# Seven waits in a two-layer decoder kernel: three asked for later or by bank, two pieces of work moved ahead, the first loads and the last stores cut anew

## The reference, cut to what matters

```python
mem_n = rmsnorm(mem, mem_norm)
for layer in range(2):
    g = norms[layer]
    h = rmsnorm(x, g[0])
    mix = even_mixer(h, ...) if layer % 2 == 0 else odd_mixer(h, ...)
    x = x + rmsnorm(mix, g[1])
    h = rmsnorm(x, g[2])
    x = x + rmsnorm(memory_cross_attention(h, mem_n, ...), g[3])
    h = rmsnorm(x, g[4])
    x = x + rmsnorm(swiglu(h, ...), g[5])
```

## Time and profile before

| | us |
|---|---|
| median of 3 executions | 2873.38 (2871.3 to 2873.62) |
| the profiled execution | 2872.75 |
| its span | 2871.0 |
| PE matmul busy | 2843.4 (99%) |
| DVE busy | 2121.0 (74%) |
| ACT busy | 1546.0 (54%) |
| POOL busy | 50.5 (2%) |
| DMA rate, mean | 203 GB/s |

### The profile page before, as it was taken

One profiled execution on the slowest core, in us unless ns is written; L12 is line 12 of the kernel. 1 busy time (PEld: TensorE's weight loads), 2 busy tenths in 40 slices (PEclk: granted clock), 3 DMA queues, 4 the chain that ended last, 5 costly groups with the idle time before them and its releaser, 6 DMA issues. The chain is left out here.

```text
span 2871.0 us, 31747 instructions
## 1 busy us (share of the span) xinstructions
PE 2843.4 (99%) x13038; PEld 2362.5 (82%) x13038; DVE 2121.0 (74%) x1453; ACT 1546.0 (54%) x1391; POOL 50.5 (2%) x102
## 2 busy tenths in 40 slices
PE   9999999999999999999999999999999999999998
PEld 7888888888888888888888888788888888888887
DVE  7888778569568988885456876669568888986444
ACT  6666555446346656664444665446446556655443
POOL 0000000000000000000000100000000000000000
PEclk9999999999999999999999999999999999999999
DMA  7674754655556456547555555655556465456552
GB/s 273 225 281 170 267 198 168 235 174 213 187 176 244 170 186 234 203 173 283 191 194 171 210 191 180 220 176 191 205 171 222 164 234 215 173 199 265 196 197 91
DMA packets 239089, 582.54 MB, mean 203 GB/s; under 512 B 8880, under 2 KB 8912, under 8 KB 223328
## 3 DMA queue, kind: packets, MB, share of 16 engines
q1 hardware_dynamic: 233616, 532.71, 52.2%
q0 software_dynamic: 4416, 37.29, 3.3%
q10 hardware_dynamic: 912, 10.50, 0.9%
HBM read 563.69 MB, written 16.78 MB: 202 GB/s over the span
## 5 line engine op out<-in xcount | busy, mean ns | idle before, releaser
L1136 DVE TENSOR_TENSOR w_lo<-wide,w_hi 128x2048 fp32r<-128x2048 f32 x548 | 1245.0, 2290 | 457.0 <-ACT w_hi L580 453.9
L580 ACT ACTIVATE w_hi<-wide 128x2048 fp32r<-128x2048 f32 x548 | 1044.8, 1914 | 499.9 <-PE ps L1833 413.9
L1833 PE MATMUL ps<-w_hi,act_hi 128*128 128x512 f32 x3352 | 897.4, 392 | 3.2 <-ACT w_hi L593 1.7
L1833 PE MATMUL ps<-w_lo,act_hi 128*128 128x512 f32 x3352 | 892.4, 390 | 0.4 <-DVE w_lo L1136 0.4
L1833 PE MATMUL ps<-w_hi,act_lo 128*128 128x512 f32 x3352 | 892.0, 390 | 0.0
L1833 PEld LDWEIGHTS ps<-w_lo,act_hi 128*128 128x128 f32 x3352 | 630.3, 188 | 131.7 <-DVE w_lo L1136 1.2
L1833 PEld LDWEIGHTS ps<-w_hi,act_lo 128*128 128x128 f32 x3352 | 630.3, 188 | 130.9
L1833 PEld LDWEIGHTS ps<-w_hi,act_hi 128*128 128x128 f32 x3352 | 627.8, 188 | 133.4 <-issue 5.5
L1140 DVE TENSOR_TENSOR wide<-wide,wide 128x2048 f32<-128x2048 f32 x102 | 233.6, 2290 | 4.7
L1091 ACT ACTIVATE act_hi<-mid 128x256 fp32r<-128x256 f32 x80 | 33.4, 418 | 243.1 <-PE ps L1833 243.1
L580 ACT ACTIVATE w_hi<-w_sum 128x2048 fp32r<-128x2048 f32 x34 | 65.3, 1922 | 100.2 <-DVE w_sum L1140 88.8
(11 more groups left out here) (253 smaller groups left out, 1570.4 us busy)
## 6 DMA issues: line engine op xcount, KB each, us to landing
wide<-in_ffn_w_gate SPq DMA_DIRECT2D x88, 1024.0 KB, 7.9
wide<-in_ffn_w_up SPq DMA_DIRECT2D x88, 1024.0 KB, 7.1
wide<-in_ffn_w_down SPq DMA_DIRECT2D x88, 1024.0 KB, 4.8
wide<-in_odd_w_in SPq DMA_DIRECT2D x48, 1024.0 KB, 5.2
wide<-in_xattn_wk SPq DMA_DIRECT2D x32, 1024.0 KB, 7.8
wide<-in_xattn_wv SPq DMA_DIRECT2D x32, 1024.0 KB, 6.6
wide<-in_even_w_in SPq DMA_DIRECT2D x32, 1024.0 KB, 6.7
wide<-in_xattn_wq SPq DMA_DIRECT2D x32, 1024.0 KB, 5.1
```

Of the source, the lines that this page charges most:

```text
L580: nc.scalar.activation(w_hi[:, c % W_SLOTS, :], src, ACT.Copy).then_inc(hi_done, 2)
L1136: nc.vector.tensor_tensor(w_lo[:, c % W_SLOTS, :], src, w_hi[:, c % W_SLOTS, :].bitcast(F32), ALU.subtract).then_inc(lo_done, 2)
L1833: return nc.tensor.matmul(dst, lhs, rhs, start=start, stop=stop, skip_group_check=loose)
```

## The change

Seven edits, in the order of the diff: the stores of the output become five parts; the start's loads are reordered (one small load moves from ACT's queue to the head of SP's, the first weight chunk goes ahead of three quarters of the memory tokens, and the second chunk waits for bank 1 in place of bank 2); `round_x` waits per bank; `take_q` on ACT goes ahead of head 0's exponentials; in the stage `gla_qk` the roots go ahead of the first token sums on DVE; `times_up` is split, its first half ahead of the split of c+1; at the end the fourth bank is scaled after the root is asked for; and on PE two waits of the even mixer are moved or taken bank by bank.

```diff
+        out_parts = [(0, slice(0, 1024)), (0, slice(1024, D)),
+                     (1, slice(0, 1024)), (1, slice(1024, 1536)), (1, slice(1536, D))]
...
                 if n == 1:
-                    sp.wait_ge(mem_in[2], 16)
+                    for b in range(1, 4):
+                        memory(b)
+                    sp.wait_ge(mem_in[1], 16)
...
-            for b in range(4):
+            def memory(b):
                 cols = slice(b * NB, (b + 1) * NB)
                 sp.dma_start(memx[:, 0, cols], mem[0:P, cols]).then_inc(mem_in[b], 16)
+            sp.dma_start(vec_rows[16:32, :], mem_norm.rearrange("(k p) -> k p", p=P)).then_inc(small_in, 16)
+            memory(0)
...
-            act.dma_start(vec_rows[16:32, :], mem_norm.rearrange("(k p) -> k p", p=P)).then_inc(small_in, 16)
...
-            def round_transposes(name, m):
+            def round_transposes(name, m, chunks=(0,) * 4):
                 pl = plan[name]
                 for b in range(4):
+                    if chunks[b]:
+                        act.wait_ge(w_used, chunks[b] + W_SLOTS)
                     act.wait_ge(work_full[WORK + b], pl["rf"] + m + 1)
...
                 def round_x():
-                    act.wait_ge(w_used, mv[1].c + SUMMED + W_SLOTS)
-                    round_transposes("pre_mix0", 0)
+                    c = mv[1].c
+                    round_transposes("pre_mix0", 0, (c + 7, c + 7, c + 10, c + 11))
...
-                    if h == 1:
+                    if h == 0:
                         take_q()
...
-                        rest8(st, nothing, other_sums, lambda: (first_sums(), before_6()))
+                        rest8(st, nothing, other_sums, lambda: (before_6(), first_sums()) if name == "gla_qk" else
+                              (first_sums(), before_6()))
...
-                def times_up():
-                    for m in range(MT):
+                def times_up(m):
...
-                lead(gu[1], before_3=times_up, before_2=lambda: token_lo(f"gu{l}"))
+                lead(gu[1], before_3=lambda: times_up(1), before_2=lambda: (token_lo(f"gu{l}"), times_up(0)))
...
                         squared()
-                        scaled_y(b, m, n)
-                    then(nc.vector.tensor_reduce(ssq[:, m:m + 1], ssq_part[:, m, :], AX_X, ALU.add))
-                    root(m)
+                        if n == 3:
+                            then(nc.vector.tensor_reduce(ssq[:, m:m + 1], ssq_part[:, m, :], AX_X, ALU.add))
+                            root(m)
+                        ins = scaled_y(b, m, n)
+                    then(ins)
...
                     pe.wait_ge(w_done, 1)
-                    for b in range(4):
-                        pe.wait_ge(bank_free[b], plan["sb_vu"]["u"] + 3)
...
                     pe.wait_ge(band_done, MT)
+                    for b in range(4):
+                        pe.wait_ge(bank_free[b], plan["sb_vu"]["u"] + 3)
...
                     pe.wait_ge(pw_in, 64)
-                    for b in range(WORK, 8):
-                        emptied(b, pl)
                     for g in range(4):
                         b = WORK + g
+                        emptied(b, pl)
```

More of the change, by code:

```diff
@@ L418, in _ @@
                     load(plan[f"down{l}"]["n"] + k, w_down[l][k * P:(k + 1) * P, :])
-            for m in range(MT):
[L421 to L425, removed]
+            for i, (m, cols) in enumerate(out_parts):
+                sp.wait_ge(x_final, i + 1)
+                sp.dma_start(out[m * P:(m + 1) * P, cols], xres[:, m, cols]).then_inc(y_out, 16)
+            sp.wait_ge(y_out, 16 * len(out_parts))
         @block.gpsimd
@@ L1305, in transposed @@
                         first_sums, other_sums = token_adds(name)
-                        rest8(st, nothing, other_sums, lambda: (first_sums(), before_6()))
-                        lead(nx, lambda: (take_t(0)(), at_lead()), before_2=lambda: token_lo(name))
+                        rest8(st, nothing, other_sums, lambda: (before_6(), first_sums()) if name == "gla_qk" else
+                              (first_sums(), before_6()))
+                        lead(nx, take_t(0), at_lead, lambda: token_lo(name))
                     else:
@@ L1748, in _ @@
                 gu = pl["strips"]
-                def times_up():
[L1751 to L1759, removed]
+                def times_up(m):
+                    dve.wait_ge(bank_free[m], gu[0].u + 2)
+                    if m == 0:
+                        dve.wait_ge(m0_done, gu[0].a + 2)
+                    else:
+                        dve.wait_ge(w_used, gu[0].c + 8 + W_SLOTS)
+                    nc.vector.scalar_tensor_tensor(out=nat[:, 0, m, :], in0=ps[:, 2 + m, :],
+                                                   scalar=rst[:, m:m + 1], in1=nat[:, 1, m, :],
+                                                   op0=ALU.mult, op1=ALU.mult).then_inc(bank_free[2 + m], 1)
                 def gather(i):
@@ L1813, in _ @@
                         squared()
-                        scaled_y(b, m, n)
-                    then(nc.vector.tensor_reduce(ssq[:, m:m + 1], ssq_part[:, m, :], AX_X, ALU.add))
-                    root(m)
-                    root_ready()
[L1818 to L1822, removed]
+                        if n == 3:
[3 more added lines that the diff above has]
+                    then(ins)
+                    root_ready()
+                    for m_out, cols in out_parts:
+                        if m_out == m:
+                            nc.vector.scalar_tensor_tensor(out=xres[:, m, cols], in0=y[:, m, cols],
+                                                           scalar=rstd[:, m:m + 1], in1=xres[:, m, cols],
+                                                           op0=ALU.mult, op1=ALU.add).then_inc(x_final, 1)
         @block.tensor
```

## The result

The changed kernel took 2857.64 us, median of five executions (2857.35 to 2858.49); the kernel before took 2873.38 us (2871.22 to 2874.1) on the same chip. The ratio is 0.9948, 95% interval 0.9934 to 0.9963. The profiled execution took 2858.27 us with a span of 2856.5, 14.5 us less than before.

A forecast was written before the change was run, and what follows sets the result against it. PE was taken as the bound, busy 2843.4 of 2871.0 us, so only its idle time counted; nine terms summed to 11.9 us, giving a forecast of 2861 us, own range 2858.5 to 2864, with A and B 2858 to 2866.

The forecast's parts named there:

- clock, layer 1: After the `times_up` idle time in layer 1, the drop to the 1.2 GHz level goes: 1.4 us, bounds 0 and 1.8.
- odd mixer, both pauses: Roots ahead of the token sums in `gla_qk`: 1.1 us for both PE losses together, bounds 0 and 2.6.
- `take_q`: Scores of head 2 no longer wait for bank 6; head 1's shares cost about 0.2: gain 0.9 us, bounds 0.5 and 1.2.
- start: Reordered loads at the start: gain 0.3 us, bounds a loss of 1.5 and a gain of 2.
- end: Root and fourth bank's scaling run side by side: 0.6 us; finer stores give nothing; bounds 0 and 0.9.
- Rival A: The waits move instead of going, across several places: gain 6.6 us, time 2866; chance 0.08.
- B: Start worse by itself, the second chunk waiting for bank 1: gain 7.4 us, time 2865.5; chance 0.07.
- C: Slower than before: memory banks trickle in at the start, clock stays at 1.2 GHz: 2879.5 us; chance 0.03.
- D: The changed waits were not what held PE, its data being late anyway: gain below 5 us, 2869; chance 0.05.
- what the first gap gives beyond that is given back there: Odd mixer: transposes at 1614.93 come 1.1 us earlier; any further gain from the first gap is lost at them.
- cover remains: At the start, ACT would split the second chunk at 14 where it did at 15.1, so its later load costs nothing.
- first reading of the prediction: Roots beside the token sums: a root gets in at the end of one such DVE instruction, and the sum stays.

The follow-up runs named there:

- c2: The changed kernel with `round_x` again waiting for c+10 to be done before all four banks: 2859.46 us.
- b4: The changed kernel with both PE waits of the even mixer as before (ahead of `sb_pv`, and all four banks ahead of `pool_map`): 2860.07 us.
- a3: The changed kernel with `times_up` in one piece again, behind the splits of c+1 and c+2: 2861.54 us.
- a1: The changed kernel with DVE's preparation of the gate back ahead of the weight sums, the roots staying ahead of the token sums: 2859.53 us.
- a2: The changed kernel with the token sums of `gla_qk` ahead of the roots again, the gate's preparation staying at its new place: 2859.06 us.
- c1: The changed kernel with `take_q` behind head 0's exponentials again: 2858.95 us.
- b2: The changed kernel with the end's order as before, the fourth bank scaled ahead of the reduction and the root: 2859.23 us.
- a4: The changed kernel with the start's loads as before, the output's five parts staying: 2858.84 us.

## Why the prediction was right, and where it failed

| step | forecast | measured |
|---|---|---|
| `round_x` | 1.6 | 1.6 (c2: 1.7) |
| `sb_pv`, `pool_map` | 2.2 | 2.1 (b4: 2.1) |
| `times_up`, both layers | 3.8 | 3.8 (a3: 3.6) |
| clock, layer 1 | 1.4 | 1.7, in one execution |
| odd mixer, both pauses | 1.1 | 2.6 (a1, a2: 1.3 each) |
| `take_q` | 0.9 | 1.0 (c1: 1.0) |
| start | 0.3 | 0.1 |
| end | 0.6 | 1.0 (b2: 1.1) |

The direction and six of the nine terms (those of `round_x`, `sb_pv`, `pool_map`, `times_up`, the clock and `take_q`) came out, as each gap of PE had one releaser, whose list could be followed. Rival A (waits that move) shows only in 0.17 us at `pool_mean`; B, C and D did not come. The forecast of the time missed by 3.4 us all the same: the spans of the two profiles differ by 14.5 us where the sum had 11.9, and the rest is where these executions lie among the others.

The term of `take_q` came out by luck. For matmuls of 128x256 I added 0.26 us to the idle time in brackets; but by their starts they follow each other every 0.216 us, with 1.255 us ahead of `pool_map` and 1.23 us ahead of the first score of head 2. So these pauses were 1.04 and 1.01 us, and not 1.14 and 1.11. Head 2's went whole (c1), and the 0.2 us that head 1's shares should take back did not come: two errors that left 0.9. The clock's term stands on one execution each, as a3 shows.

The step that failed is "what the first gap gives beyond that is given back there", and with it the sign that the transposes 21 us later still wait over 1 us: they wait for nothing. It was right for the kernel that I had in mind (a1 loses the 1.34 us there) and wrong for the change, because I read its line for the order of roots and sums and not for the arguments of `lead` below it. The upper bound that I gave, 2.6, is what was measured. The end was mis-sized: the order's 0.6 us on DVE was 0.5, but from the last store's issue to the end it is also 0.6 us less, and the third store, which I put at nothing, costs 0.4 in the new order. At the start two errors cancel: the clock rose at 12.1, 5.5 us sooner than in the profile before, and the wait on SP, whose "cover remains" was wrong, took that back. I had ACT splitting the second chunk at 14 (it was 14.26) and left out that PE, at the 2.4 GHz level, would want it at 14.7.

## What to carry to other kernels

In a kernel whose main engine is busy 99% of the time, list its pauses, follow the list of the engine that ends each, and ask what is late next; here six of nine such terms held to 0.3 us. Read every argument that a diff's line changes, not only what its title says. At the start, these runs favour an order of the loads that leaves the matmul engine no pause directly ahead of its first long product (why is argued, not shown), and no wait that holds the following load back.

## What the runs showed of the hardware

- An idle time of 3.2 us ahead of the first long product was followed by a fall of the clock from the 2.4 to the 1.2 GHz level at 12.07 (a4), which it had reached at 8.66 on transposes alone; after 3.3 us of idle time ahead of twelve transposes it rose at 12.1 (changed kernel). In the middle of the kernel 2.06 us of idle time were followed by 3.4 us at the lower level once, and 1.70 us were not.
- A root of 0.56 us on GpSimd took 0.92 us beside a DVE addition of two SBUF operands and ended 0.4 us after that addition, not after all four; beside DVE's scaling out of PSUM it took 0.54. This agrees with the first reading of the prediction. The Trainium skill (SBUF — State Buffer, "SBUF: two separate sides") names as contending a DVE instruction with two SBUF inputs and a GpSimd one that reads SBUF; these times agree.
- Three stores in place of two for the last 1 MB made the end 0.4 us later in the new order (8.25 against 7.84 us from the last matmul), and 0.07 us in the old one (9.36 against 9.29).
